# Router logits from 32-column weight pieces in four column groups of TensorE, folded by a selector product

## The reference, cut to what matters

```
u = x * (1.0 + sc2) + sh2
aff = softmax((u @ router_w).astype(f32), axis=-1)      # router_w is (1024, 16)
```

## Time and profile before

| | |
|---|---|
| time, median of 3 | 1422.11 us (1419.53 to 1424.17) |
| the profiled execution's own time | 1419.87 us |
| its span, first to last instruction | 1418.1 us |
| mean granted TensorE clock | 0.941 |
| TensorE matmul busy | 1281.8 us, 90% of the span |
| VectorE, ScalarE, GpSimd busy | 1080.4, 776.0, 291.0 us |
| the 128 router instructions of L1028 | 27.0 us busy, in two stages: 234.4 to 254.3 us and 1026.4 to 1046.0 us |

### The profile page before, as it was taken

One profiled execution on the slowest core, in us unless ns is written; L12 is line 12 of the kernel. 1 busy time (PEld: TensorE's weight loads), 2 busy tenths in 40 slices (PEclk: granted clock), 3 DMA queues, 4 the chain that ended last, 5 costly groups with the idle time before them and its releaser, 6 DMA issues.

```text
span 1418.1 us, 18543 instructions
## 1 busy us (share of the span) xinstructions
PE 1281.8 (90%) x6679; PEld 1004.7 (71%) x6680; DVE 1080.4 (76%) x1213; ACT 776.0 (55%) x1006; POOL 291.0 (21%) x324
## 2 busy tenths in 40 slices
PE   4999999499999999889898999999948999999985
PEld 4867778377777777568886777757747777777762
DVE  7787867688898898569956677653758888889857
ACT  3423223277777777464434555665225777777760
POOL 0112215110000000235004455544141000000020
PEclk8999997599999999999979999999958999999998
DMA  9877872199999999905403333225316999999971
GB/s 358 310 274 271 302 255 104 48 352 406 388 387 389 393 393 396 328 15 185 138 1 119 105 105 106 72 91 192 133 66 245 403 385 390 380 382 394 396 280 76
DMA packets 109644, 355.01 MB, mean 250 GB/s; under 512 B 7792, under 2 KB 16220, under 8 KB 109546
## 3 DMA queue, kind: packets, MB, share of 16 engines
q1 hardware_dynamic: 87688, 277.91, 52.3%
q0 software_dynamic: 17296, 60.38, 12.1%
q10 hardware_dynamic: 4594, 15.84, 2.7%
HBM read 329.94 MB, written 25.21 MB: 250 GB/s over the span
## 4 chain that ended last, share of the span: by engine, by line
PE 49%; issue 19%; DVE 15%; ACT 9%; DMA 6%; POOL 2%; ACTq 1%; SPq 0%; DVEq 0%; POOLq 0%
PE bank L235 11%; PE bank L236 10%; PE bank L237 10%; ACT w_hi L1243 3%; DMA ada<-in_ada_w_dram 3%; PE bank L2088 2%; DVE acc L463 2%; PE bank L2070 2%; POOL prob L2309 2%; DMA xg<-scratch_u,tok 1%; PE bank L1028 1%; ACT w_hi L225 1%; PE bank L1190 1%; PE bank L2058 1%; DVE w_lo L230 1%
## 5 line engine op out<-in xcount | busy, mean ns | idle before, releaser
L1249 DVE TENSOR_TENSOR w_lo<-raw,w_hi 128x2048 fp32r<-128x2048 f32 x189 | 437.0, 2317 | 71.3 <-ACT w_hi L1243 69.3
L1243 ACT ACTIVATE w_hi<-raw 128x2048 fp32r<-128x2048 f32 x189 | 362.5, 1918 | 85.6 <-PE bank L237 75.2
L235 PE MATMUL bank<-w_lo,xe_hi 128*128 128x512 f32 x512 | 212.0, 414 | 9.3 <-DVE xe_lo L1206 9.2
L237 PE MATMUL bank<-w_hi,xe_hi 128*128 128x512 f32 x512 | 203.8, 398 | 0.0
L236 PE MATMUL bank<-w_hi,xe_lo 128*128 128x512 f32 x512 | 203.7, 398 | 0.0
L1179 POOL DMA_INDIRECT xg<-scratch_u,tok x32 | 36.1, 1128 | 555.0 <-DVE tok L1173 554.3
L230 DVE TENSOR_TENSOR w_lo<-raw,w_hi 128x2048 fp32r<-128x2048 f32 x37 | 87.5, 2368 | 60.5 <-ACT w_hi L225 60.3
L225 ACT ACTIVATE w_hi<-raw 128x2048 fp32r<-128x2048 f32 x37 | 70.6, 1909 | 109.8 <-PE bank L237 83.2
L2309 POOL TENSOR_SCALAR prob<-prob,rsum,gates 128x512 f32<-128x512 f32 (+3 forms) x128 | 108.5, 861 | 90.9 <-DVE rsum L2277 90.9
L235 PE MATMUL bank<-u_lo,w_hi 128*128 128x512 f32 x288 | 118.9, 413 | 9.1 <-DVE q L1975 4.2
L235 PEld LDWEIGHTS bank<-w_lo,xe_hi 128*128 128x128 f32 x512 | 97.3, 190 | 39.1 <-issue 10.8
(11 more groups left out here) (313 smaller groups left out, 2452.4 us busy)
## 6 DMA issues: line engine op xcount, KB each, us to landing
raw<-in_w_gu_dram SPq DMA_DIRECT2D x128, 1024.0 KB, 7.9
raw<-in_w_down_dram SPq DMA_DIRECT2D x64, 1024.0 KB, 8.7
ada<-in_ada_w_dram POOLq DMA_DIRECT2D x48, 512.0 KB, 6.8
ada<-in_ada_w_dram SPq DMA_DIRECT2D x32, 512.0 KB, 3.8
scratch_y<-ye ACTq DMA_DIRECT2D x30, 512.0 KB, 7.4
raw<-in_conv_w_in_dram SPq DMA_DIRECT2D x12, 1024.0 KB, 13.5
mod_w<-in_ada_w_dram SPq DMA_DIRECT2D x8, 1024.0 KB, 14.0
raw<-in_w_kv_dram SPq DMA_DIRECT2D x6, 1024.0 KB, 9.5
```

The source lines that it names most:

```text
L235: nc.tensor.matmul(o, lh, rl, start=start, stop=False)
L237: return nc.tensor.matmul(o, lh, rh, start=False, stop=stop)
L1243: nc.scalar.activation(w_hi[:, hslot, :], raw[:, slot, :], ACT.Copy).then_inc(hi_done, 1)
L1249: nc.vector.tensor_tensor(w_lo[:, slot, :], raw[:, slot, :], w_hi[:, hslot, :].bitcast(F32), ALU.subtract).then_inc(lo_done, 1)
```

## The change

The router product swaps its operands. The weights become the stationary operand, padded from 16 to 32 columns with zeros, and the tokens `u_t[:, k, t]` (128 columns) the moving one. Chunk k is written to PSUM partitions 32q to 32q+31 with q = k mod 4, so that four chunks stand in four column groups and each group adds up two chunks. ScalarE copies the 128x128 piece of partial logits (transposed, four partial sums) to `lgt`. A second small product with `lgt` stationary and a 128x16 selector `fold` (made once from the identity) adds the four groups and turns the result to token rows; the product with ones and `rwb_sum` goes before it. The order in the streams changes: `part_act` (the copy) stands in ScalarE's stream between `norm_apply` and `turn_act` of later tiles, and the last one before `split_hi`; TensorE does router(i), transposes(i+1), logits(i). The first router product waits for residual 7 of 8 (`TT + 3`) in place of residual 5, for its PSUM banks.

```
@@ front_act
             for i in range(TT):
                 norm_root(act, s.ln0, i)
                 norm_apply(act, s.ln0, i)
+                if i >= 2:
+                    part_act(act, s, i - 2)
                 if i >= 1:
                     turn_act(act, s.turn, u_t, i - 1)
+            part_act(act, s, TT - 2)
             turn_act(act, s.turn, u_t, TT - 1)
+            part_act(act, s, TT - 1)
             split_hi(act, b0 + 3 + NSPLIT)
@@ front_dve
-            nc.vector.tensor_tensor(rws[:], rw[:], bc(acol[:], [P, KD, NE], 2), ALU.mult).then_inc(s.pre.sem, 1)
+            dve.wait_ge(*s.pre.at(2))
+            link(dve, dve_n, dve_step, nc.vector.memset(rws[:], 0.0))
+            nc.vector.tensor_tensor(rws[:, :, 0:NE], rw[:], bc(acol[:], [P, KD, NE], 2), ALU.mult).then_inc(s.pre.sem, 1)
@@ buffers
-        rws = at("rws", [P, KD, NE], F32, U0 + 13 * KB + 512)
+        rws = at("rws", [P, KD, 2 * NE], F32, U0 + 13 * KB + 512)
+        lgt = at("lgt", [P, 2, P], F32, S0 + 20 * KB)
@@ router_pe
             if i == 0:
                 pe.wait_ge(*s.pre.at(3))
-                pe.wait_ge(*s.rwb_made.at(1))
-                pe.wait_ge(*proj.res.at(TT + 1))
-            o = bank[s.proj_banks[4]][:, i * NE:(i + 1) * NE]
+                pe.wait_ge(*proj.res.at(TT + 3))
+            if i >= 2:
+                pe.wait_ge(*s.part_copied.at(i - 1))
             t = slice(i * P, (i + 1) * P)
-            nc.tensor.matmul(o, ones_col[:, 0:1].to_broadcast([P, P]), rwb_sum[:], start=True, stop=False)
             for k in range(KD):
                 if k % 4 == 0:
                     pe.wait_ge(*s.turn.hi.at(2 * i + k // 4 + 1))
-                m = nc.tensor.matmul(o, u_t[:, k, t], rws[:, k, :], start=False, stop=(k == KD - 1))
-            if i == TT - 1:
-                m.then_inc(s.logit.sem, 1)
+                q = k % 4
+                m = nc.tensor.matmul(bank[s.proj_banks[5 + i % 2]][32 * q:32 * (q + 1), 0:P], rws[:, k, :], u_t[:, k, t],
+                                     start=(k < 4), stop=(k >= 4), skip_group_check=True)
+            m.then_inc(s.part_made.sem, 1)
+
+        def logits_pe(pe, s, proj, i):
+            if i == 0:
+                pe.wait_ge(*s.rwb_made.at(1))
+                pe.wait_ge(const_v, FOLD_MADE)
+            pe.wait_ge(*s.part_copied.at(i + 1))
+            o = bank[s.proj_banks[4]][:, i * NE:(i + 1) * NE]
+            nc.tensor.matmul(o, ones_col[:, 0:1].to_broadcast([P, P]), rwb_sum[:], start=True, stop=False)
+            m = nc.tensor.matmul(o, lgt[:, i % 2, :], fold[:], start=False, stop=True)
+            m.then_inc(s.logit.sem, 1)
+
+        def part_act(act, s, i):
+            act.wait_ge(*s.part_made.at(i + 1))
+            if i >= 2:
+                act.wait_ge(*s.logit.at(i))
+            nc.scalar.activation(lgt[:, i % 2, :], bank[s.proj_banks[5 + i % 2]][:, 0:P], ACT.Copy
+                                 ).then_inc(s.part_copied.sem, 1)
@@ front_pe
-            router_pe(pe, s, proj, 0)
-            for i in range(1, TT):
-                turn_pe_plain(pe, s.turn, xt[:, i, :], i)
+            for i in range(TT):
                 router_pe(pe, s, proj, i)
+                if i + 1 < TT:
+                    turn_pe_plain(pe, s.turn, xt[:, i + 1, :], i + 1)
+                logits_pe(pe, s, proj, i)
@@ start of the VectorE stream, once, before the convolution
-            dve.wait_ge(const_v, 3)
+            nc.vector.tensor_reduce(fold[:], ident[:].rearrange("p (q e) -> p e q", q=4)[:, 0:NE, :], AX_X, ALU.add
+                                    ).then_inc(const_v, 1)
+            dve.wait_ge(const_v, FOLD_MADE)
```

More of the change, by code:

```diff
@@ L129, in hybrid_trunk @@
         eps_col = new("eps_col", [P, 1], F32)
+        fold = new("fold", [P, NE], F32)
         ones_b = new("ones_b", [P, P], BF16)
@@ L288, in hybrid_trunk @@
         N_CONST = 6
+        FOLD_MADE = 4
         class AdaPass:
@@ L962, in hybrid_trunk @@
         rw = at("rw", [P, KD, NE], F32, U0 + 13 * KB)
-        rws = at("rws", [P, KD, NE], F32, U0 + 13 * KB + 512)
-        rwb = at("rwb", [P, KD, NE], F32, U0 + 13 * KB + 1024)
-        rwb_sum = at("rwb_sum", [P, NE], F32, U0 + 13 * KB + 1536)
+        rws = at("rws", [P, KD, 2 * NE], F32, U0 + 13 * KB + 512)
+        rwb = at("rwb", [P, KD, NE], F32, U0 + 13 * KB + 1536)
+        rwb_sum = at("rwb_sum", [P, NE], F32, U0 + 15 * KB)
+        lgt = at("lgt", [P, 2, P], F32, S0 + 20 * KB)
         aff = rnew("aff", [P, TT, NE])
@@ L994, in __init__ @@
                 self.rwb_made, self.exp_in, self.expd, self.chose, self.posd = once.values()
-                self.listed, self.logit = Count("moe_listed", 3), Count("moe_logit", 2)
+                self.listed, self.logit = Count("moe_listed", 3), Count("moe_logit", 1 + TT)
+                self.part_made, self.part_copied = Count("moe_comb", TT), Count("moe_gated", TT)
                 self.end_ready = Count("moe_end_ready", 2)
@@ L1051, in route_dve @@
             full, grp = [P, TT, NE], [P, TT, NG]
-            dve.wait_ge(*s.logit.at(2))
+            dve.wait_ge(*s.logit.at(1 + TT))
             if s.l == 0:
```

## The result

After the change the kernel takes 1413.0 us (1411.8 to 1416.2), against 1422.1 before (1419.5 to 1424.9): a ratio of 0.9938, 95% interval 0.9923 to 0.9953. It is 9.1 us faster. The prediction was 1419.6, its range began at 1415.8, and "faster" had 0.22. It was wrong.

What follows compares the result with a forecast made beforehand. TensorE's router products of tiles 1 and 2, delaying tile 3's transposes before `split_hi`, were taken to bound both fronts; gains of 1.4 and 1.1 us took 1422.1 to 1419.6 us, range 1415.8 to 1426.0.

Steps and rivals of the forecast that it cites:

- The two rivals on overlap: Router blocks: only pairs overlap, 2.7 us slower, chance 0.13; or no overlap among 32-column pieces, 13 us slower, chance 0.12.
- costed at nothing: Side edits such as the `rws` memset (some 0.25 us), selector and later residual wait, all expected covered by idle time.
- the idle time ahead of VectorE's earlier `split_lo`: VectorE's 0.73 us wait for ScalarE, said to cover the memset; otherwise at most 0.4 us a layer.
- the size of r: One router block's time at half clock: 1.43 us for tiles 1 and 2, 1.09 for tile 3.
- ScalarE copy: After tile 2's `norm_apply`, copying tile 0's partial logits adds 0.35 us to the path.
- three logits steps: Ones and fold products between router blocks on TensorE: 0.86 us each, 2.58 us on the path.
- transposes of tiles 2, 3: TensorE's transposes of two tiles on the path: 2 x 1.74, 3.48 us.
- three router blocks: Router products of three tiles on the path, four column groups side by side: 3.95 us in all.
- end: Before `split_hi`: 0.18 us until the last result is readable plus 0.30 for tile 3's copy, 0.48 us.
- the switching price: Changing TensorE between full and divided array around a router block: 0.24 us entry, 0.34 exit at half clock.
- The nearest rival: Router blocks run four groups side by side without switching price, r 0.85 us, gain 5.3 us; chance 0.20.
- without overlap the change would lose 13 us: Router blocks with no overlap among 32-column pieces: 7.7 us more a layer, 13 us slower overall; chance 0.12.

Runs made afterwards that it cites:

- one_group: Changed kernel with all eight 32-column pieces of a tile in one column group, selector taking the first group alone: 1414.8 us, ratio 0.9946.
- old_warm: Kernel before, with 14 bf16 products of 384 streamed columns ahead of each layer's first router block: 1419.7 us, ratio 0.9973.
- old_wide: Kernel before, with every router column streamed eight times (128 columns instead of 16), same loads and order: 1416.8 us, ratio 0.9966.
- old_wide_pad: Kernel before, with router columns streamed eight times and twelve 16-column dummy products per layer ahead of the first router block: 1412.1 us, ratio 0.9925.
- both_warm: Changed kernel, logits steps behind the last router block, `split_hi` before the last copy, 14 filling 384-column products before the first router block: 1413.1 us, ratio 0.9938.
- old_pad2: Kernel before, with twelve 16-column bf16 dummy products per layer ahead of the first router block: 1420.1 us, ratio 0.9983.
- after_pad: Changed kernel, with 14 16-column bf16 dummy products per layer ahead of the first router block: 1412.6 us, ratio 0.9933 to the kernel before.
- split_first: Changed kernel with ScalarE's `split_hi` moved ahead of its last copy of partial logits: 1413.2 us, ratio 0.9928 to the kernel before.

## Why the prediction was wrong

**What held.** The path was read rightly: `split_hi` in either layer is what the routing waits for, the router blocks of tiles 1 and 2 delay it, and the new chain goes step by step as laid out. Four column groups do run side by side: a half-clock block went from 3.41 to 1.01, its four rounds of 0.213 and 0.16 more. The two rivals on overlap had their conditions refuted by that row. Nothing costed at nothing became visible: the memset takes 0.27 us, and the idle time ahead of VectorE's earlier `split_lo` shrank from 0.73 to 0.23 in layer 0, as the cover it was said to be. The token stores and the gather kept out of the way. So did GpSimd's multiplications, but by 0.59 us only; that they were the next floor, the prediction did not see.

**The step that failed first: the size of r (one router block) and of the logits step.** With the measured chain in place of the forecast one, layer 0's 10.84 us becomes 8.77 and layer 1's becomes 8.94:

| term | forecast | layer 0 | layer 1 |
|---|---|---|---|
| ScalarE copy | 0.35 | 0.31 | 0.31 |
| three logits steps | 2.58 | 1.01 + 0.67 + 0.36 | 1.01 + 0.67 + 0.35 |
| transposes of tiles 2, 3 | 3.48 | 1.90 + 1.46 | 1.90 + 1.68 |
| three router blocks | 3.95 | 1.01 + 1.01 + 0.85 | 1.01 + 1.01 + 0.81 |
| end | 0.48 | 0.20 | 0.19 |

The blocks were forecast 1.1 us a layer too dear: I doubled the switching price seen at full clock (0.12 and 0.17) to 0.24 and 0.34 because the clock was half. Measured from start to start at half clock (241.38, 241.89 and 242.91 us for the fold product, the block and the transposes), a block takes 1.02, that is 0.17 over its four rounds, as much as at full clock, and the product ahead of it 0.51 in place of 0.43, 0.08 more. A logits step that follows transposes takes 0.67, not 0.86, as the chain gives the product with ones only 0.24 behind them; three steps were 0.5 a layer too dear. `split_hi` came 3.5 and 3.0 us sooner, 6.4 together, 3.9 more than forecast: 2.2 from the blocks, 1.1 from the logits steps, 0.6 from the end, next to nothing from the rest. The nearest rival was the one without a switching price (5.3 us), to which I gave 0.20, and it falls 1.1 us short as well. That four groups work side by side was taken over from two without a row of its own, and came true.

The Trainium skill (TensorE: Matmul & The Clock Gate, Part 3) lets a load overlap running products only where the row groups differ. The trace disagrees: here all pieces share all rows, and the sixteen instructions, each with its load, still take 1.01, where one group alone takes 3.47 (first line of one_group's timeline).

**The step that failed as a thought: the clock was taken as given.** "The granted clock in this stretch is 0.50, so these are prices at 1.2 GHz" went into both sides of the sum. But what clock the front gets also hangs on what the front issues. In that stretch TensorE had work in flight for 9.58 of 10 us and still ran at half. old_warm shows that the old front loses the clock even if it is entered with it; old_wide shows that with the same loads and 128 streamed columns it comes back (239.5 us in layer 0); and old_wide_pad, that this and the missing stand together are worth as much as the whole change. In the changed kernel the clock shows directly only in the last part of the chain: about 0.8 us in layer 0 (0.44 in the transposes, 0.31 in the logits step) and 0.5 in layer 1, some 1.3 of the 3.9 us by which the forecast was short. Beyond that, column groups and full clock are two ways to the same place, the floor that GpSimd sets. A block of 3.5 to 3.8 us from first start to last end falls to 1.08 at half clock with four groups, and to 1.93 or 2.05 at full clock with none; and a full clock shortens the transposes too. The forecast compared only "groups or nothing" at a fixed clock, and so held that without overlap the change would lose 13 us. It gained 6.5 in one_group.

The Trainium skill (TensorE: Matmul & The Clock Gate, Part 1) ties the granted clock to how busy the array has been. The profile's busy share is not that measure: 9.58 of 10 us busy, and 0.50 granted. What the engine did before its clock fell or rose is what old_warm, both_warm and old_wide show.

**The term that was missing: the end of the kernel.** 2.1 us are the last stretch, 1.85 of them the stand at the last combine. The stand has nothing to do with the router: 24 dummy products take it away from the kernel before (old_pad2), 28 more bring it back to the changed one (after_pad). In the medians this is at the edge of what can be told: old_pad2 is 1.6 us faster, and after_pad no slower than the changed kernel. No line of the diff points to it; in the profile of before it was a single row, "issue" 1.85 us.

**The sum:** forecast gain 2.5; fronts 6.7; last stretch 2.1; together 8.8, where the profiled executions differ by 7.9 and the medians by 9.1. Even without the stand the time would have been about 1415, just below the range.

**What stays open.** What TensorE waits for at the combine: the trace names no releaser, and a reading of it as late instructions fits but was only argued. What moved split_first and old_wide by 3 us from their terms. How much of the changed kernel's own front is the clock: a run that holds it at half with the new products was not made. And what a front does with less work on GpSimd: no run moved that work, so its floor rests on the 13 stages alone.

## What to carry to other kernels

Before a stretch is costed, look at its granted clock and ask which of the removed or added work keeps it there: here a front of weight loads with 16-column moving operands sat at 1.2 GHz with TensorE hardly ever idle, and widening the stream to 128 columns, even with copies that nobody reads, shortened it more than the restructuring did (8.0 against 6.7 us). Then look for the next floor: the engine off the path that ends closest ahead of the next step (here GpSimd, 4.07 us ahead) bounds what any change to TensorE can give. If a change both swaps operands and adds parallelism, run the swap alone. And for effects under 0.3%, compare a landmark-to-landmark table over the whole span, not only the changed stage: adding a few instructions can move a 2 us stand somewhere else, so the same edit with some dummy instructions is a fair second sample.

## What the hardware showed that I had not expected

- Sixteen float32 instructions of 16 columns with 128-column loads: 3.59 us at half clock, 1.96 at full (old_warm). Sixteen of 128 columns: 3.60 and 1.93 with 32-column loads (one_group), 3.79 and 2.05 with 128-column loads (old_wide, layers 1 and 0). Eight times the streamed columns cost 0.2 us at half clock and 0.1 at full.
- The clock rose behind 128-column blocks (237.2 us in one_group, 239.5 in old_wide) and did not behind the 16-column blocks of the kernel before. It fell behind a 16-column block with hardly a wait (1030.6 in old_warm), and behind two 128-column blocks with a wait of 3.32 us between them (240.8 in both_warm).
- Four column groups of 32: sixteen instructions in 1.01 us at half clock, switching included.
- VectorE's `split_lo`, 2.29 us by itself, takes up to 3.88 when it starts under a GpSimd multiplication: it ends 2.14 to 2.16 us behind that one's end in all 13 cases.
- A stand of 0.9 to 2.2 us on TensorE at one product comes and goes with the number of instructions ahead of it, the last added ones of which were issued some 350 us before.
